# Seven edits to the order of work in a fused three-layer block on one core, one of them the engine that empties the differential heads' output bank

## The reference, cut to what matters

```python
def reference(x, c, w_ada, ..., dil_w_out_2):
    x = first_block(x, c, ...)    # sparse_indexer_attention, 8 heads; gated conv; layer_norm; swiglu; layer_norm
    return second_block(x, p_2, ...)

def second_block(x, p, ...):
    h = x
    for i in range(2):
        hn = rms_norm(h, norm_mix[i])
        mix = gla_mixer(hn, ...) if i == 0 else diff_attn_mixer(hn, ...)
        h = h + mix
        h = h + swiglu_2(rms_norm(h, norm_ffn[i]), ffn_w_in[i], ffn_w_out[i])
        gate = jax.nn.sigmoid(rms_norm(h, ple_norm[i]) @ ple_w_gate[i])
        h = h + gate * (p[i] @ ple_w_proj[i])
    return h

# differential attention, 8 heads h, two score maps t = 0, 1 per head
s = einsum(q_blk, kt) * scale
pr = softmax(s)
a = pr[:, :, 0] - lam * pr[:, :, 1]
o = einsum(a, vt)                       # 128 columns per head
o = rms_norm(o, g_sub) * (1 - lambda_init)
return o.reshape(...) @ w_out

# gated linear attention: the gates come from a narrow product
q, k, v, r, zf, zb = split_cols(h @ w_in, [512, 512, 1024, 1024, 16, 16])
la_f = log_sigmoid(zf @ w_gate_f + b_gate_f) / GLA_TAU
```

## Time and profile before

| | us |
|---|---|
| median of three runs | 1086.41 |
| the profiled execution | 1086.66 |
| its span, first to last instruction | 1084.9 |
| TensorE busy | 1045.9 (96%) |
| VectorE busy | 731.6 (67%) |
| ScalarE busy | 553.1 (51%) |
| GpSimd busy | 207.5 (19%) |
| mean granted TensorE clock | 0.991 of full speed |

### The profile page before, as it was taken

How to read it: one execution, slowest core, us unless ns; L and a number is a source line. 1 busy time by engine, 2 the same in 40 slices (tenths; PEclk the granted TensorE clock), 3 DMA queues, 4 the chain that set the end, 5 groups by cost and what they waited for, 6 DMA issues and landing times.

```text
span 1084.9 us, 20420 instructions
## 1 busy us (share of the span) xinstructions
PE 1045.9 (96%) x7985; PEld 983.2 (91%) x7985; DVE 731.6 (67%) x1155; ACT 553.1 (51%) x946; POOL 207.5 (19%) x227
## 2 busy tenths in 40 slices
PE   5999998999999999999999999999998999999998
PEld 5677787999999988989999999998976999999998
DVE  5697767676745786768656655686787766564565
ACT  2223466544554594527645443566566764454443
POOL 0000013323321101013233320121210223332010
PEclk9999999999999989999999999999999999999999
DMA  9993452577656544602655456663330464644661
GB/s 351 400 373 125 155 195 78 175 240 260 208 155 185 165 155 155 215 20 91 220 187 200 133 153 179 243 223 134 123 133 3 154 233 157 219 141 128 193 208 40
DMA packets 183587, 192.78 MB, mean 178 GB/s; under 512 B 5913, under 2 KB 143426, under 8 KB 183522
## 3 DMA queue, kind: packets, MB, share of 16 engines
q1 hardware_dynamic: 182512, 191.15, 52.0%
q0 software_dynamic: 144, 0.52, 0.2%
q10 hardware_dynamic: 866, 0.21, 0.1%
HBM read 190.83 MB, written 1.05 MB: 177 GB/s over the span
## 4 chain that ended last, share of the span: by engine, by line
PE 56%; DVE 5%; ACT 3%; issue 1%; POOL 0%; DVEq 0%; POOLq 0%; ACTq 0%
PE gemm L2205 16%; PE gemm L2207 16%; PE gemm L2206 16%; DVE wlo L1461 1%; PE aux L2693 1%; ACT whi L897 1%; PE aux L2813 1%; PE aux L2743 1%; PE aux L2205 1%; DVE prod L1935 1%; PE aux L2207 1%; PE aux L2206 1%; PE gemm L2796 0%; PE aux L2749 0%; DVE state L2061 0%
## 5 line engine op out<-in xcount | busy, mean ns | idle before, releaser
L1461 DVE TENSOR_TENSOR wlo<-raw,whi 128x1024 fp32r<-128x1024 f32 (+1 forms) x308 | 353.4, 1191 | 62.5 <-ACT whi L897 61.8
L2205 PE MATMUL gemm<-ohi,whi 128*128 128x256 f32 x1376 | 389.1, 283 | 3.7 <-issue 1.1
L2206 PE MATMUL gemm<-olo,whi 128*128 128x256 f32 x1376 | 386.6, 281 | 0.0
L2207 PE MATMUL gemm<-ohi,wlo 128*128 128x256 f32 x1376 | 384.7, 280 | 0.0
L897 ACT ACTIVATE whi<-raw 128x1024 fp32r<-128x1024 f32 (+1 forms) x308 | 276.5, 963 | 59.6 <-PE gemm L2207 47.5
L2205 PEld LDWEIGHTS gemm<-ohi,whi 128*128 128x128 f32 x1376 | 259.8, 189 | 7.3 <-issue 3.2
L2206 PEld LDWEIGHTS gemm<-olo,whi 128*128 128x128 f32 x1376 | 259.9, 189 | 0.6 <-issue 0.5
L2207 PEld LDWEIGHTS gemm<-ohi,wlo 128*128 128x128 f32 x1376 | 259.9, 189 | 0.0
L2207 PE MATMUL gemm<-acthi,wlo 128*128 128x256 f32 x528 | 147.7, 280 | 0.0
L2205 PE MATMUL gemm<-acthi,whi 128*128 128x256 f32 x528 | 147.7, 280 | 0.0
L2206 PE MATMUL gemm<-actlo,whi 128*128 128x256 f32 x528 | 147.3, 279 | 0.0
(11 more groups left out here) (379 smaller groups left out, 1558.1 us busy)
## 6 DMA issues: line engine op xcount, KB each, us to landing
raw<-in_ffn_w_in SPq DMA_DIRECT2D x44, 1024.0 KB, 6.7
raw<-in_ffn_w_out SPq DMA_DIRECT2D x32, 704.0 KB, 5.3
part<-in_w_ada SPq DMA_DIRECT2D x32, 512.0 KB, 9.5
raw<-in_gla_w_in SPq DMA_DIRECT2D x6, 2048.0 KB, 8.4
raw<-in_diff_w_in SPq DMA_DIRECT2D x6, 2048.0 KB, 8.0
raw<-in_w_gate SPq DMA_DIRECT2D x11, 1024.0 KB, 6.3
raw<-in_w_up SPq DMA_DIRECT2D x11, 1024.0 KB, 8.5
raw<-in_w_down SPq DMA_DIRECT2D x16, 704.0 KB, 5.5
```

The source lines that it names most:

```text
L1461: dve.tensor_tensor(wlo[hslot][:, q * w:(q + 1) * w], src[:, q * w:(q + 1) * w], whi[hslot][:, q * w:(q + 1) * w].bitcast(F32), ALU.subtra ...
L2205: pe.matmul(dst, st_hi, mv_hi, start=start, stop=False)
L2206: pe.matmul(dst, st_hi, mv_lo, start=False, stop=False)
L2207: return pe.matmul(dst, st_lo, mv_hi, start=False, stop=stop_)
```

## The change

Seven edits. None changes what is computed, the number of matmuls or the data moved.

1. Differential heads. VectorE's copy of a head's output (8 copies of 128x256) goes to ScalarE as `take_head`, in turn i between the four exponentials of head i and the copy of head i-1's turned probabilities. `out2`'s slab quarters are made in turns 1 to 4 (before: 3, 4, 5 and 7), their low parts in turns 2 to 5. At the end TensorE turns head 7 before it multiplies head 6, and the third group's statistics go behind the first step of `out2`.
2. First attention: VectorE takes head 0's maxima before the low parts of `out0`, two of which go into heads 1 and 2.
3. First attention: ScalarE squares the convolution's first half before it splits a quarter of `out0`, in turn 6.
4. `out0`, second slab: VectorE makes the last low quarter after the last tile's addition instead of before it.
5. Start of the gated linear attention: VectorE takes one bank of the side projection, the squares, another bank, and the other two only after `g_z` (semaphore `pp_late`); TensorE's statistics and narrow product stand before the last tile of `gla_q` instead of behind it.
6. `gla_v`: the exponentials of the second direction move from behind the first slab to the middle of the second.
7. `gla_v`, second slab: all four quarters of the next slab before the first tile's evacuation.

```diff
@@ quarters, quarter_between (edits 7 and 4)
-            if first and ph.name in WIDE:
+            if first and ph.name in WIDE or ph.name == "gla_v":
                 each = (4, 0, 0, 0)
...
+            if ph.name == "out0" and not act:
+                return {0: (1,), 1: (2,), 3: (3,)}.get(t, ())
@@ ScalarE, beside_head (edit 3)
+                if i == 6:
+                    group_squares(2, gated_ready, 2)
                 if i in (5, 6):
                     split(PH["out0"], At(1), i - 5)
                 if i == 6:
-                    group_squares(2, gated_ready, 2)
                     high_parts(0, 1)
@@ ScalarE, gla_after (edit 6)
-                if at.i == 0 and t == 1:
-                    for d in range(2):
+                if (at.i, t) in ((0, 1), (1, 0)):
+                    for d in (at.i,):
@@ ScalarE, differential heads (edit 1)
+            def take_head(h):
+                act.wait_ge(pv_done, NH + h + 1)
+                act.activation(tl(d_o, h), X[2][:, 0:T], ACT.Copy).then_inc(mixed_ready, 1)
...
                         me.did(ins, exp_done)
+                if i >= 3:
+                    take_head(i - 3)
                 if i == 5:
                     squares((0,), d_o, d_nsq)
+                if i == 7:
+                    pair_root(0, X[1])
+                    squares((1,), d_o, d_nsq)
                 if i >= 1:
                     me.next(trans_done)
...
-                    if i >= 3:
-                        act.wait_ge(pv_done, NH + i - 2)
                     me.did(act.activation(tl(d_pt, (i - 1) % 2, w=512), X[0][:, :], ACT.Copy), pt_ready)
                 if i in (2, 5, 7):
                     take_values({2: 1, 5: 2, 7: 3}[i])
-                if 3 <= i <= 5 or i == 7:
-                    ahead(*OUT2, min(i - 3, 3))
...
+                if 1 <= i <= 4:
+                    ahead(*OUT2, i - 1)
             wait(act, tile_done, PH["diff_v"].tile0 + 4)
+            take_head(6)
             high_parts_of(0, 1)
+            pair_root(1, X[1])
             squares((2,), d_o, d_nsq)
-            pair_root(1, X[1])
+            take_head(7)
@@ VectorE, first attention (edit 2)
-            for q in range(4):
+            masked_maxima(0)
+            for q in range(2):
                 low(PH["out0"], At(0), q)
             modulate_part(10)
-            masked_maxima(0)
...
+                if i in (1, 2):
+                    low(PH["out0"], At(0), i + 1)
@@ VectorE, side projection and squares (edit 5)
-            for n, copies in pp_copies(1):
...
+            take_projection(2, pp_ready[0])
             SQUARED = 4
...
+            take_projection(3, pp_ready[0])
+            dve.wait_ge(z_hi_ready, 1)
+            dve.tensor_tensor(z_lo[:, :], ...)
             for q in range(3):
                 low(PH["gla_k"], At(0), q)
             root()
...
+            for n in range(2):
+                take_projection(n, pp_late)
@@ VectorE, differential heads (edit 1)
-                if i >= 3:
-                    me.next(pv_done)
-                    me.did(dve.tensor_copy(tl(d_o, i - 3), X[2][:, 0:T]), mixed_ready)
...
-                if 4 <= i <= 6 or i == 8:
-                    low(*OUT2, min(i - 4, 3))
+                if 2 <= i <= 5:
+                    low(*OUT2, i - 2)
@@ TensorE, gla_q (edit 5)
+            def sums_and_gates(at, t):
+                if t != 2:
+                    return
+                stats(tok=True, summed=gla_summed)
+                ...
+                ins.then_inc(z_done, 1)
+            gemm("gla_q", dve_read, olo_from=start, after=sums_and_gates)
@@ TensorE, differential heads (edit 1)
             for i in range(NH + 2):
                 if i + 1 < NH:
                     scores(i + 1)
+                if 2 <= i < NH:
+                    attend(i - 2)
                 if i < NH:
                     value_steps(16 + 6 * i, 22 + 6 * i)
+                if 1 <= i <= NH:
+                    transposes(i - 1)
                 if i in (6, 8):
                     group_stats((i // 2 - 3,), ones[:, :], d_nsq, X[1:2])
+                if i >= NH:
+                    attend(i - 2)
```

More of the change, by code:

```diff
@@ L1931, in add @@
                 def add(t):
-                    if t == 0:
-                        dve.wait_ge(pp_ready[k - 1], 4)
+                    if t == 0 and k == 1:
+                        dve.wait_ge(pp_ready[0], 2)
+                        dve.wait_ge(pp_late, 2)
+                    elif t == 0:
+                        dve.wait_ge(pp_ready[1], 4)
                     dve.wait_ge(ple_sig, KT * (k - 1) + t + 1)
@@ L1959, in _, with take_projection @@
             layer_norm(1)
-            for n, copies in pp_copies(1):
+            def take_projection(n, ready):
                 dve.wait_ge(pp_done, n + 1)
-                for dst, bank in copies:
+                for dst, bank in dict(pp_copies(1))[n]:
                     ins = dve.tensor_copy(dst, bank)
-                ins.then_inc(pp_ready[0], 1)
-            dve.wait_ge(z_hi_ready, 1)
-            dve.tensor_tensor(z_lo[:, :], raw[PH["gla_z"].slot][:, 0:384], z_hi[:, :].bitcast(F32),
-                              ALU.subtract).then_inc(z_lo_ready, 1)
+                ins.then_inc(ready, 1)
+            take_projection(2, pp_ready[0])
             SQUARED = 4
@@ L2145, in low_pair @@
                     me.did(low_part(t, tl(om, t), xhi, xlo), olo_ready)
-            for i in range(NH + 3):
+            for i in range(NH + 2):
                 if i < NH:
@@ L2174, in _ @@
                     me.did(ins, prob_ready)
-                if i == NH + 1:
+                if i == NH:
                     wait(dve, tile_done, PH["diff_v"].tile0 + 4)
                     make_pair(0)
-                if i == NH + 2:
+                if i == NH + 1:
                     low_pair(0)
@@ L2538, in projection_of @@
                     if t % 2 == 0:
-                        banks.claim(bank, pp_ready[n])
+                        banks.claim(bank, pp_late if (n, t < 4) == (0, True) else pp_ready[n])
                     for k in range(2):
@@ L2635, in _ @@
             start = next_operand()
-            gemm("gla_q", dve_read, olo_from=start)
-            stats(tok=True, summed=gla_summed)
-            pe.wait_ge(z_lo_ready, 1)
-            banks.claim(X[1], z_ready)
-            for k in range(KT):
-                ins = three(X[1][0:48, 0:T], z_hi[:, 48 * k:48 * (k + 1)], z_lo[:, 48 * k:48 * (k + 1)], tl(ohi, k),
-                            tl(olo, k), k == 0, k == KT - 1)
-            ins.then_inc(z_done, 1)
+            def sums_and_gates(at, t):
+                if t != 2:
+                    return
+                stats(tok=True, summed=gla_summed)
+                pe.wait_ge(z_lo_ready, 1)
+                banks.claim(X[1], z_ready)
+                for k in range(KT):
+                    ins = three(X[1][0:48, 0:T], z_hi[:, 48 * k:48 * (k + 1)], z_lo[:, 48 * k:48 * (k + 1)], tl(ohi, k),
+                                tl(olo, k), k == 0, k == KT - 1)
+                ins.then_inc(z_done, 1)
+            gemm("gla_q", dve_read, olo_from=start, after=sums_and_gates)
             pe.wait_ge(z_ready, 1)
@@ L2802, in _, with attend, transposes @@
             scores(0)
+            def attend(h):
+                banks.claim(X[2], mixed_ready)
+                me.next(pt_ready)
+                if h % 2 == 0:
+                    pe.wait_ge(v_ready, 4 + h // 2 + 1)
+                for kt in range(2):
+                    ins = pe.matmul(X[2][:, 0:T], d_v[:, kt * D + h * P:kt * D + (h + 1) * P],
+                                    tl(d_pt, h % 2, w=512)[:, kt * T:(kt + 1) * T], start=(kt == 0), stop=(kt == 1))
+                ins.then_inc(pv_done, 1)
+            def transposes(h):
+                s = h % 2
+                banks.claim(X[0], pt_ready)
+                me.next(prob_ready)
+                for kt in range(2):
+                    for qt in range(2):
+                        ins = pe.transpose(X[0][:, kt * T + qt * P:kt * T + (qt + 1) * P],
+                                           tl(d_p, 4 * s + qt)[:, kt * P:(kt + 1) * P], ident)
+                ins.then_inc(trans_done, 1)
             for i in range(NH + 2):
@@ L2805, in _ @@
                     scores(i + 1)
[L2806 to L2815 removed]
+                if 2 <= i < NH:
+                    attend(i - 2)
                 if i < NH:
                     value_steps(16 + 6 * i, 22 + 6 * i)
+                if 1 <= i <= NH:
+                    transposes(i - 1)
                 if i in (6, 8):
                     group_stats((i // 2 - 3,), ones[:, :], d_nsq, X[1:2])
[L2820 to L2830 removed]
+                if i >= NH:
+                    attend(i - 2)
             start = next_operand()
             gemm("out2", dve_read, olo_from=start, operand=(xhi, xlo),
[L2833 removed]
+                 beside={0: lambda: group_stats((2,), ones[:, :], d_nsq, X[0:1]),
```

(1 more changed line is left out.)

28 lines of the change are left out of this document (3 added, 25 removed).

## The result

The changed kernel takes 1093.49 us (median of 8 runs, 1092.02 to 1100.25), the kernel before 1086.42 (8 runs): the ratio is 1.0067, 95% interval 1.0048 to 1.0087. The profiled execution took 1094.52 us, 7.86 more than that of before; its span is 1092.7 and its mean granted clock 0.988 (before 0.991).

The account below looks back on a forecast made before the run. TensorE, busy 1045.9 of 1084.9 us, was taken to bound the kernel. 1086.7 - 4.6 (edits 2 to 7) + 11.2 (edit 1) + 5.0 (clock) = 1098.3, less 0.3 for the median: 1098 us; range 1091 to 1104.

Parts of the forecast that it names:

- the ring: Differential heads: turning, probabilities copy, exponentials, output copy, output product, values steps, next turning; 6.55 us against 4.69; edit 1 +11.2 us.
- the 4.9 of that place: Differential heads: head 1's output product starts at 817.0 instead of 812.09, so 4.9 us late.
- Clock in the gaps: Differential heads: TensorE idles five times for 2.1 to 3.2 us; four falls to half clock at 1.25, +5.0 us.
- The Trainium skill's rule: TensorE's clock: idle gaps below a given length leave it untouched; the heads' clock term would be zero, the time 1093.
- Edit 2 (-0.5): First attention: the 2.4 us wait for masked scores shrinks to 0.6, but VectorE paces the next three heads: -0.5 us.
- Edit 3 (-0.6): First attention: square put first frees 0.95 of the 1.3 us wait, the later quarter gives back 0.35: -0.6 us.
- Edit 4 (-1.8): `out0`, layer norm sums: GpSimd's wait falls from 1.8 to 1.0 us, full clock gives another 1.0: -1.8 us.
- Edit 5 (-0.9): Gated linear attention's start: gates start earlier, `gla_k` waits for a low quarter, starts at 396.8 before 397.7: -0.9 us.
- Edits 6 and 7 (-0.8): `gla_v` to `gla_r`: fourth low quarter ends about 1.3 us before needed, so the 0.8 wait goes: -0.8 us.
- The clock holds: Rival, differential heads: clock stays full through the gaps, 1098 - 5 = 1093 us; chance 0.24.
- The faster rival: Differential heads: output copy done before TensorE asks, VectorE loses eight copies, late waits go; 1078 us; chance 0.04.
- the point named for it: Differential heads: exponentials' wait for the turned probabilities; they would have to start a turn before it.

Follow-up runs that it names:

- The two experiments that opened the ring at either of two links: Changed kernel with ScalarE's output copy right behind the copy of turned probabilities: 1080.10 us; changed kernel with TensorE's values steps ahead of the output product: 1079.01 us.
- the late quarters: Changed kernel with the four quarters of `out2`'s slab back in turns 3, 4, 5 and 7: 1095.20 us, ratio 1.0066.
- once the ring was open: Changed kernel with ScalarE's output copy behind the turned probabilities and `out2`'s slab quarters in turns 2, 3, 4 and 6: 1075.56 us, ratio 0.9891.
- the filled turns: Changed kernel with TensorE making the scores of heads 4 to 7 three times over into the same bank: 1091.03 us, ratio 1.0040.
- the heads alone: Kernel before with the edit of the differential heads (edit 1) alone: 1099.74 us, ratio 1.0116.

## Why the prediction was right, and which sizes were off

The forecast was 1098 us, slower, by a ring on ScalarE; 1093.49 came, slower, by that ring. Of the 4.5 us between them the clock made 2.0 (too much), the six small edits 1.5 (too little gain) and the ring 0.4 (too much), all with the same sign; the rest is that the profiled executions lie 7.9 apart and the medians 7.1.

- **Edit 1, the ring (+11.2 predicted).** Right link by link: 0.64, 0.49, 1.80, 0.45 and 3.10 against 0.63, 0.50, 1.79, 0.53 and 3.10; the last of the four turns, with nothing else in it, 6.51 against 6.6. (The end of the two `d_v` copies is 812.34 in the trace, not 812.35, and 10.1 + 0.9 + 0.3 is 11.3, not 11.2: neither matters.) Head 1's product came at 811.04, which with the 6.1 gained upstream is 817.1 on the clock of before, predicted 817.0. `out2` began 12.7 late against the shift upstream, less 3.0 of half clock 9.7 (predicted 10.1), and the statistics in it cost 1.1 (1.2): +10.8. The two experiments that opened the ring at either of two links, and the one that took the copy to VectorE, each with the rest of edit 1 in place, show that the ring turns a gain into the loss. The first quarter in turn 1 cost something besides: 2.6 of the +5.2 at head 1's product, by the late quarters, and 3.6 in the heads once the ring was open. The forecast had it in the 4.9 of that place.
- **Clock in the gaps (+5.0 predicted).** This is the term that was mis-sized: it measured 3.0 by the filled turns, 2.5 by the medians. The step that failed is "most of the new gaps should be followed by half speed". Of the five gaps one, that which ends at 820.02, had a fall behind it; the one that ends at 811.04 already lay in half clock, from a fall behind the wait for head 2's exponentials; behind the last three the clock was full. After gaps of 2.67 and 2.66 us it fell once and once it did not, in the same execution; the earlier trace rows gave one gap with a fall and one shorter one without, and I made the length between them into what decides. The two stretches cost 1.5 each, near the 1.25 of the forecast; their number was wrong. The Trainium skill's rule that I cited ("TensorE: Matmul & The Clock Gate", section "HAM oscillation — how this bites in real kernels"), by which such short gaps leave the clock alone, is also contradicted: the clock fell to 0.50 behind waits of 1.91 and 2.67 us, and where the gap of 2.67 was filled down to 0.94 it stayed full.
- **Edit 2 (-0.5): -0.6.** The reason given, that VectorE is next in line, holds, and the trace of after shows it: the wait for scores became 0.7, the clock did not fall at 89, and still all but 0.6 of it was given back at the turnings of heads 0, 2 and 3 (the forecast had the new waits at heads 0 and 1). ScalarE's scaled probabilities are named there, but they wait for VectorE's reciprocal, which comes right behind two low parts and a modulation sum:

```profile
88.14 2.35 DVE L1471 TENSOR_TENSOR wlo<-out_w,whi 128x1024 fp32r<-128x1024 f32 x2
90.41 1.53 DVE L1570 SCALAR_TENSOR_TENSOR acc_c<-part,c_act,acc_c 128x512 f32<-128x512 f32 x2
91.98 0.17 DVE L1721 RECIPROCAL rsum<-sums 128x2 f32<-128x2 f32 x1
```

- **Edit 3 (-0.6): -0.6.** At the group's statistics 0.9 had been gained (136.41 and 134.88, shift -1.5); 0.3 of it was gone at head 7's turning, as worked out.
- **Edit 4 (-1.8): -2.4.** GpSimd's last two instructions took 0.73 and 0.72, without a low quarter beside them (the earlier trace rows had 1.54 for the first), and the sum products began 0.8 sooner, as predicted. The clock stayed full, which gave 1.7 and not 1.0: all of the 3.4 us at half speed were work on the path, and half of 3.4 is what they cost.

```profile
167.94 0.73 POOL L820 TENSOR_TENSOR mean<-mean,res 128x256 f32<-128x256 f32 x1
168.62 0.72 POOL L822 TENSOR_TENSOR sq_sum<-sq_sum,ln_sq 128x256 f32<-128x256 f32 x1
```

- **Edit 5 (-0.9): -0.9 at the start of `gla_k`, -1.4 behind the half clock;** that the first figure met the forecast is luck. The gates began at 389.2, 5.2 sooner than before. The half clock, 6.8 us long in both executions, then covers 2.1 us of the gates (391.07 to 393.12) and before it covered 0.9 (396.83 to 397.69), so the gates lost 0.6 by it and `gla_k` won about as much. They ended at 393.1, just as the fourth low quarter was done, and the wait of 0.6 for that quarter, which I had forecast, does not appear.
- **Edits 6 and 7 (-0.8): -1.1.** The wait for a low quarter is gone, as predicted; the rest is not attributed.
- **The sum.** Upstream -6.1 for -4.6, ring +10.8 for +11.2, clock +3.0 for +5.0: 7.7 for 11.6, and 7.8 in the span. The experiment with the six edits alone gives -5.4 by medians; its interval, -7.6 to -4.5, holds both -6.1 and -4.6. Terms read from one execution carry the clock of that execution: the six edits' own profile has -7.7 where this one has -6.1.
- **The rivals.** "The clock holds" gave 1093, the nearest number, by luck: the clock did not hold (3.0 instead of 0), and the six edits brought 1.5 more than it reckoned; the two errors have opposite signs and cancel in part. The faster rival failed at the point named for it, the exponentials' wait. TensorE waited for the output copy at six of the seven products that need one; only that of head 6 found it done.

## What to carry to other kernels

Before an instruction that releases a buffer goes to another engine, write down the ring that it joins: from the release through everything in front of it in the new queue, back to the release. If this loop is longer than the pace of the bounding engine, each turn waits for the difference (1.9 us where the ring was 6.51 and the pace 4.69). That an engine is busy half of the time, as ScalarE with 51% here, says nothing about it. The place in the queue was worth 13 us here and the engine nothing measurable; a slab quarter ahead of an instruction that is waited for cost 2 to 4; a ring can be opened on either side, by moving the release ahead of unrelated work or the waiting engine's own filler ahead of its wait.

## What the runs showed of the hardware

Idle gaps of the same length did not treat TensorE's clock alike. In the changed kernel the granted clock was 0.51 after the gap of 2.67 us that ends at 820.02 and 1.00 after that of 2.66 which ends at 828.97; in the heads alone, with gaps of 2.67 at the same two products, it was the other way round. Behind the wait of 1.91 for head 2's exponentials the clock fell with the copy behind the turned probabilities (0.50 from 805.8 to 809.1) and did not with the copy on VectorE (1.00 from 805.9 to 809.3). And with the order of before in the heads, where the longest waits are 1.51 and 1.60 us, it stayed at 1.00 in the kernel before and was 0.50 from 832.6 to 839.3 in that with the six small edits. What decides was not tested.

The profiles of thirteen kernels show mean granted clocks from 0.984 to 0.998, and runs of one and the same kernel differ by up to 0.010: the changed kernel took 1092.38 us at 0.993 and 1100.25 at 0.983. So the clock's part of a forecast can be given as a cost of one fall (1.5 us here) times a chance, not as a count. And a stretch of half clock may cost nothing: that at 89.6 went with edit 2, and almost none of its time came back, because VectorE set the pace there.
